# The context vector's lane of the modulation's multiply-adds: from VectorE to GpSimd, as a multiply and an add

## The reference

```python
for l in range(DEPTH):
    mod = silu_c @ w_mod[l] + b_mod[l]
    shift, scale, gate = jnp.split(mod[:, None, :], 3, axis=-1)
    cmod = silu_cc @ w_mod[l] + b_mod[l]
    cshift, cscale, cgate = jnp.split(cmod, 3)
    h = rmsnorm(x, norm_g[l]) * (1.0 + scale) + shift
    hc = rmsnorm(cx, norm_g[l]) * (1.0 + cscale) + cshift
    ...                      # projections, two attention mixers, gate, output projection
    x = x + gate * (y @ w_o[l])
    if with_ctx:
        cx = cx + cgate * (yc @ w_o[l])
```

## Time and profile before

| | |
|---|---|
| median of 3 runs | 2505.77 us (2504.22 to 2507.44) |
| profiled execution | 2506.52 us |
| its span, first to last instruction | 2504.7 us |
| mean granted TensorE clock | 0.992 |
| TensorE matmul busy | 2398.6 us (96%) |
| VectorE busy | 1527.2 us (61%) |
| ScalarE busy | 1033.8 us (41%) |
| GpSimd busy | 232.0 us (9%) |

### The profile page before, as it was taken

How to read it: one execution, slowest core, us unless ns; L and a number is a source line. 1 busy time by engine, 2 the same in 40 slices (tenths; PEclk the granted TensorE clock), 3 DMA queues, 4 the chain that set the end, 5 groups by cost and what they waited for, 6 DMA issues and landing times. The chain is left out here.

```text
span 2504.7 us, 31388 instructions
## 1 busy us (share of the span) xinstructions
PE 2398.6 (96%) x11660; PEld 1919.8 (77%) x11660; DVE 1527.2 (61%) x2575; ACT 1033.8 (41%) x1712; POOL 232.0 (9%) x329
## 2 busy tenths in 40 slices
PE   6899999999999999999899999999999999999998
PEld 1467787877667878887777788978878888899886
DVE  1247766677777877857746556666576544444664
ACT  3232232334343322333353445444544445654543
POOL 0001101001110000002121100100110001101100
PEclk9999999999999999999999999999999999999999
DMA  9756644434333475666465464755655566567653
GB/s 342 283 207 237 211 144 151 167 128 152 103 116 135 143 246 166 202 204 214 158 202 165 129 201 156 263 183 189 201 166 186 185 207 220 169 201 232 191 193 127
DMA packets 231174, 467.96 MB, mean 187 GB/s; under 512 B 17642, under 2 KB 42536, under 8 KB 229744
## 3 DMA queue, kind: packets, MB, share of 16 engines
q1 hardware_dynamic: 209104, 394.94, 47.7%
q0 software_dynamic: 21920, 71.01, 8.8%
HBM read 435.10 MB, written 30.79 MB: 186 GB/s over the span
## 5 line engine op out<-in xcount | busy, mean ns | idle before, releaser
L2091 PE MATMUL pp<-w_hi,hT_hi 128*128 128x512 f32 (+3 forms) x2904 | 1171.0, 403 | 6.7 <-DVE xy L1521 2.8
L2093 PE MATMUL pp<-w_hi,hT_lo 128*128 128x512 f32 (+3 forms) x2904 | 1116.5, 384 | 0.0
L2092 PE MATMUL pp<-w_lo,hT_hi 128*128 128x512 f32 (+3 forms) x2904 | 1114.4, 384 | 0.0
L1491 DVE TENSOR_TENSOR w_lo<-raw,w_hi 128x1024 fp32r<-128x1024 f32 (+4 forms) x570 | 671.9, 1182 | 579.9 <-ACT w_hi L1213 578.6
L1213 ACT ACTIVATE w_hi<-raw 128x1024 fp32r<-128x1024 f32 (+4 forms) x570 | 580.2, 1023 | 446.3 <-PE pp L2093 373.8
L2091 PEld LDWEIGHTS pp<-w_hi,hT_hi 128*128 128x128 f32 x2904 | 547.9, 189 | 136.4 <-issue 38.1
L2093 PEld LDWEIGHTS pp<-w_hi,hT_lo 128*128 128x128 f32 x2904 | 546.6, 188 | 105.8
L2092 PEld LDWEIGHTS pp<-w_lo,hT_hi 128*128 128x128 f32 x2904 | 548.5, 189 | 94.7 <-issue 6.9
L1591 DVE SCALAR_TENSOR_TENSOR arena<-raw,cT,arena 128x512 f32<-128x512 f32 x240 | 172.3, 745 | 0.7
L1591 DVE SCALAR_TENSOR_TENSOR xy<-raw,cT,xy 128x512 f32<-128x512 f32 x180 | 126.7, 744 | 0.0
L1372 ACT ACTIVATE arena<-pY 128x512 f32<-128x512 f32 (+2 forms) x114 | 62.0, 544 | 146.0 <-PE pY L2252 109.0
(11 more groups left out here) (305 smaller groups left out, 1753.0 us busy)
## 6 DMA issues: line engine op xcount, KB each, us to landing
raw<-in_w_mod_dram SPq DMA_DIRECT2D x192, 512.0 KB, 5.3
raw<-in_w_in_dram SPq DMA_DIRECT2D x168, 512.0 KB, 4.2
raw<-in_e_w_in_dram SPq DMA_DIRECT2D x104, 512.0 KB, 4.6
raw<-in_w_o_dram SPq DMA_DIRECT2D x64, 512.0 KB, 4.6
raw<-in_o_w_in_dram SPq DMA_DIRECT2D x64, 512.0 KB, 4.7
raw<-in_w_out_dram SPq DMA_DIRECT2D x64, 512.0 KB, 4.1
raw<-in_w_in_dram SPq DMA_DIRECT2D x56, 440.0 KB, 3.9
scratch_u<-ust POOLq DMA_DIRECT2D x35, 512.0 KB, 4.3
```

Of the source, the lines that this page charges most:

```text
L1491: dve.tensor_tensor(w_lo[:, g.s % SPLIT, 0:n], raw[:, g.n % RAW, 0:n], w_hi[:, g.s % SPLIT, 0:n].bitcast(F32), ALU.subtract).then_inc(lo_d ...
L2091: pe.matmul(dst, hT_hi[:, kk, o:o + P], hi[:, k, :], start=a, stop=False)
L2092: pe.matmul(dst, hT_hi[:, kk, o:o + P], lo[:, k, :], start=False, stop=False)
L2093: ins = pe.matmul(dst, hT_lo[:, kk, o:o + P], hi[:, k, :], start=False, stop=z)
```

## The change

For lane 1 the mac leaves VectorE. GpSimd does it with two instructions: it multiplies the raw K tile in place by the context's column of `cT`, waits for that, and adds the product to the running sum of lane 1 (or to `parts` with K = 0). Since the multiply destroys the raw tile, GpSimd first waits for VectorE's mac of lane 0 on the same tile. Each lane has a semaphore and a count of its own; SP, `bias`, `fold` and `fold_row` wait for both or for the lane that they read. The slots in the plan stay as they are, so the macs of lane 1 stand in GpSimd's queue where they stood in VectorE's. The chunks with lane 0 only stay as they were.

```diff
--- before.py
+++ after.py
@@ -687,10 +687,10 @@
     for todo in plan.at:
         for e in todo:
             if e[0] == "mac":
-                mac_n[e[1:]] = len(mac_n) + 1
+                mac_n[e[1:]] = sum(k[2] == e[3] for k in mac_n) + 1
     side_n = {ch.name: n for n, ch in enumerate(W.sides)}
     for g in W.sided:
-        mac_end[g] = max(mac_n[g.ch.name, K, v] for K in g.ks for v in g.ch.lanes)
+        mac_end[g] = {v: mac_n[g.ch.name, g.ks[-1], v] for v in g.ch.lanes}
     acc_before = {}
     for n, ch in enumerate(W.sides):
         same = [c for c in W.sides[:n] if c.acc == ch.acc]
@@ -779,7 +779,7 @@
         fl_here, fl_added, fl_logged, fl_min, fl_stored = (sem(n) for n in ("fl_here", "fl_added", "fl_logged", "fl_min", "fl_stored"))
 
         cb_here = [sem(f"cb_here{n}") for n in range(2)]
-        parts_clear, side_bias, maced = sem("parts_clear"), sem("side_bias"), sem("maced")
+        parts_clear, side_bias, multiplied, maced = sem("parts_clear"), sem("side_bias"), sem("multiplied"), [sem(f"maced{v}") for v in range(2)]
 
         def at(o, *shape):
             n = int(np.prod(shape))
@@ -858,9 +858,9 @@
             key = ("fold", ch.name, 1) if ch.row is None else ("fold_row", ch.name)
             return filled["O"], left["O", key]
 
-        def maced_all(ch, v=None):
-
-            return maced, max(mac_n[ch.name, ch.ks[-1], w] for w in ch.lanes if v in (None, w))
+        def maced_all(ch, v):
+
+            return maced[v], mac_n[ch.name, ch.ks[-1], v]
 
         def heads_before(m, n):
             return plan.heads[plan.H[m, n].qi - 1] if plan.H[m, n].qi else None
@@ -970,7 +970,8 @@
                     if p.ch.kind == "mod":
                         sp.wait_ge(quanta, p.q1)
                     elif p.ch.kind == "side":
-                        sp.wait_ge(maced, mac_end[p])
+                        for v, n in mac_end[p].items():
+                            sp.wait_ge(maced[v], n)
                     else:
                         sp.wait_ge(lo_done, p.s + 1)
                 ch = g.ch
@@ -1016,10 +1017,34 @@
                 ch, n = C[name], side_n[name]
                 if n:
                     prev = W.sides[n - 1]
-                    pool.wait_ge(maced, mac_n[prev.name, 0, prev.lanes[-1]])
+                    for v in prev.lanes:
+                        pool.wait_ge(maced[v], mac_n[prev.name, 0, v])
                 else:
                     pool.wait_ge(parts_clear, 1)
                 pool.dma_start(parts[0:1, :], D["b_mod"][ch.layer:ch.layer + 1, ch.c0:ch.c0 + 512]).then_inc(side_bias, 16)
+
+            def mac(name, K, v):
+                if v != 1:
+                    return
+                ch = C[name]
+                g = ch.groups[K // GROUP]
+                acc, n = accs[C[name].acc][:, v, :], mac_n[name, K, v]
+                if K % GROUP == 0:
+                    pool.wait_ge(raw_here[g.n % RAW], 16 * (g.n // RAW + 1))
+                if K == 0:
+                    pool.wait_ge(side_bias, 16 * (side_n[name] + 1))
+                    if acc_before[name] is not None:
+                        pool.wait_ge(*folded(acc_before[name]))
+                    elif ch.acc == 2:
+                        pool.wait_ge(*freed_from(plan.U["b", 7, 3].X, ("score", "b", 7, 3)))
+                else:
+                    pool.wait_ge(maced[v], mac_n[name, K - 1, v])
+                k = K % GROUP
+                part = raw[:, g.n % RAW, 512 * k:512 * k + 512]
+                pool.wait_ge(maced[0], mac_n[name, K, 0])
+                pool.tensor_scalar(part, part, cT[:, K, 1:2], None, ALU.mult).then_inc(multiplied, 1)
+                pool.wait_ge(multiplied, mac_n[name, K, 1])
+                pool.tensor_tensor(acc, part, parts[:, :] if K == 0 else acc, ALU.add).then_inc(maced[1], 1)
 
             def gate_store(name):
                 ch = C[name]
@@ -1182,6 +1207,8 @@
                         clear()
                     elif name == "bias":
                         bias(*key)
+                    elif name == "mac":
+                        mac(*key)
                     elif name == "gate":
                         gate(*key)
                     elif name == "tables":
@@ -1574,10 +1601,12 @@
                     scaled_gain(name, key)
 
             def mac(name, K, v):
+                if v != 0:
+                    return
                 ch = C[name]
                 g = ch.groups[K // GROUP]
                 acc, n = accs[C[name].acc][:, v, :], mac_n[name, K, v]
-                if K % GROUP == 0 and v == 0:
+                if K % GROUP == 0:
                     dve.wait_ge(raw_here[g.n % RAW], 16 * (g.n // RAW + 1))
                 if K == 0:
                     dve.wait_ge(side_bias, 16 * (side_n[name] + 1))
@@ -1586,10 +1615,10 @@
                     elif ch.acc == 2:
                         dve.wait_ge(*freed_from(plan.U["b", 7, 3].X, ("score", "b", 7, 3)))
                 else:
-                    dve.wait_ge(maced, mac_n[name, K - 1, v])
+                    dve.wait_ge(maced[v], mac_n[name, K - 1, v])
                 k = K % GROUP
                 dve.scalar_tensor_tensor(acc, raw[:, g.n % RAW, 512 * k:512 * k + 512], cT[:, K, v:v + 1], parts[:, :] if K == 0 else acc,
-                                         ALU.mult, ALU.add).then_inc(maced, 1)
+                                         ALU.mult, ALU.add).then_inc(maced[v], 1)
 
             def sums(name, n):
                 if name == "a":
@@ -2113,8 +2142,8 @@
 
             def fold_row(name):
                 b = begin("O", "fold_row", name)
-                pe.wait_ge(*maced_all(C[name]))
                 for v in C[name].lanes:
+                    pe.wait_ge(*maced_all(C[name], v))
                     ins = pe.matmul(b[32 * v:32 * v + 1, :], ones_mat[:, 0:1], accs[C[name].acc][:, v, :], start=True, stop=True)
                 ins.then_inc(filled["O"], 1)
```

## The result

The changed kernel takes 2621.82 us (median of 4 runs, 2619.25 to 2628.84) against 2505.75 us before: a ratio of 1.0467, 95% interval 1.0446 to 1.0489, or +116 us. The forecast was 2556 us with a range of 2500 to 2650: the sign and the mutual lock held, the time lies in the range, but the loss is 2.3 times what I worked out.

What follows compares the result with a forecast made beforehand. TensorE, 96% busy, was taken to bound the kernel. Window losses of +6, +26, +10 and +8 us gave +50 on the profiled 2506.5 us, 2556.5; the forecast was 2556 us, range 2500 to 2650.

Steps and rivals of the forecast that it cites:

- What bounds the kernel, and the relief: TensorE, 96% busy, sets the end; VectorE loses 129 us of macs, worth at most 10 us on the path.
- The multiply's price: GpSimd's multiply of 128x512: between 0.53 and 0.92 us, taken as 0.7; with an add of 1.2, a pair costs 1.9.
- dear pairs: Rival, chance 0.12: a GpSimd multiply and add cost 2.9 us together, making +153 us, 2659 us.
- its sign: GpSimd's new lines taking 2.5 us or more in mean would show the upper end due.
- The sum by windows: GpSimd pairs, lane 0 macs and splits can't overlap: +6 (163-202 us), +26 (202-268), +10 (268-808), +8 (808-1030).
- The lock, symmetric: GpSimd's reading multiply or add holds off VectorE's macs and splits for up to its whole length, as VectorE does GpSimd.
- Lateness between 268 and 808 us: Attention steps of VectorE start up to 1.2 us late; half of TensorE's 21.5 us idle time added, +10.
- Folds: TensorE's fold of lane 1 comes 2.7 us after the last mac was due; GpSimd's backlog stops TensorE there, 12 times.
- The clock: TensorE's granted clock is 0.99 to 1.00 everywhere, the 2.4 GHz level, so it plays no part.
- Only late, not locked: Rival, chance 0.20: VectorE is never held up, only GpSimd runs late; about +17, 2523 us.
- faster: Rival, chance 0.10: a pair under 1.45 us, the lock costs little, half of 20 us of waits go; 2496 us.
- nothing moves: Rival, chance 0.08: gain and loss cancel within 5 us; 2506 us.

Runs made afterwards that it cites:

- e_free: Changed kernel without lane 1's multiply and add; GpSimd writes eight zeros per tile (512 for K = 0), waits kept: 2493.06 us, 0.9949 of the kernel before.
- e_add_only: Changed kernel without the multiply; GpSimd adds the raw tile itself to lane 1's running sum: 2518.73 us, 1.0044 of the kernel before.
- e_tt_mul: Changed kernel with GpSimd's multiply as a two-input tensor_tensor against the broadcast column of cT: 2596.79 us, 1.0355 of the kernel before.
- e_light: Changed kernel with only four chunks' lane 1 (64 tiles, slots 227 to 435) on GpSimd, the rest on VectorE: 2520.47 us, 1.0048 of the kernel before.
- e_light_memset: Only four chunks (64 tiles, slots 227 to 435) moved, with five zero-writing memsets per tile replacing multiply and add: 2503.11 us, 0.9992 of the kernel before.
- e_memset: Changed kernel with five zero-writing GpSimd memsets per tile replacing lane 1's multiply and add, waits kept: 2548.07 us, 1.0161 of the kernel before.

## Why the prediction went wrong

*What bounds the kernel, and the relief.* Right: TensorE sets the end, and VectorE's relief (120 us, taken as 129) was worth 13 us (10 predicted), shown by `e_free`.

*The multiply's price.* This is the step that failed. I bounded it by a memset and by a memset plus the fixed part of a power op, 0.53 to 0.92 us, and took 0.7; it measured 1.57. Both bounds rest on the pace of writing, and GpSimd's time for an element depended on the operation's form: 1.57, 1.04 and 1.27 us for three instructions on the same 512 elements. With the range of 0.9 to 1.97 for the add the sum's upper end, 2.9 us a pair, took in the measured 2.84 by luck of the add's end, so the case that came true was the one I had called dear pairs, at 0.12 and 2659 us; its sign, 2.5 us or more in mean, came with 1.78 + 1.43. That the price makes the difference between 50 and 116 us is borne out by two runs: `e_add_only` with 1.27 us of instructions a tile lost 10 us and `e_tt_mul` with 2.31 lost 89, which puts my 1.9 us near 60 (an interpolation between kernels whose instructions differ).

*The sum by windows.* With 2.84 in place of 1.9 us my own terms give 14 x 2.84 + 18 - 39 = +19, 31 x 2.84 + 33.6 - 66 = +56, 244 + 314 - 540 + 10 = +28, and 173 + 88 - 222 = +39, in all +142; measured were 0, 42, 34 and 44, +119. So the form of the sum held from the second stretch on. It failed in the first, where I had +6 even at 1.9 us and nothing was lost, and it was too strict for the first two together (+75 against 42): a window's work can be done later than it is due. GpSimd has done 39 of the 45 tiles at 311 us, and the other six are paid in the next stretch, where 91 pairs lie instead of 86.

*The lock, symmetric.* Right that both sides stand, by the rows at 217 us, by `e_light` against `e_light_memset` and by `e_memset` against the change. Too simple in its length: the sum gave every pair its whole length as time in which VectorE stands, and beside the multiply VectorE went on after about 0.5 of 1.57 us. (The trace of before has 24 power ops, not 23; the last, at 2495 us, took 1.10 us where others of its size took 0.71, and fits the same reading.) The lock costs in two ways, which by the interpolations above come to this: it makes GpSimd's pairs longer on the steep part of the curve (3.0 to 3.4 us in the change, some 40 us; 2.5 to 2.9 in `e_tt_mul`, some 20), and it holds up VectorE (some 28 and 49 us). Which is the larger depends on the instructions, and neither was measured by itself.

*Lateness between 268 and 808 us, +10.* Too low: 34 us. 17.3 of it is one wait for the first rotation, whose load and whose weight split both came late by the backlog that the dense window left; I had costed loads behind pairs at nothing. Some of the rest is the lock's (64 tiles: 13 us in `e_light`).

*Folds.* Right in kind: of the twelve, seven waited for GpSimd, 43 us, and one for VectorE, 12 us.

*The clock.* Left out; 33 us of TensorE's longer busy time. It isn't a cause of its own but a surcharge on the idle stretches.

*The rivals.* "Only late, not locked" is refuted by `e_light` against `e_light_memset`, "faster" by the time and, where GpSimd has room, by `e_light`, "nothing moves" by the time.

## What to carry to other kernels

Price a GpSimd instruction by its own form and shape, not by a neighbour's: a scalar multiply of 128x512 cost 1.57 us there, the same as a two-input product 1.04, and VectorE did product and sum together in 0.67. Before work is moved to an idle engine, divide its price by the spacing at which the work is due; near 100% the loss grew here by about 100 us for a microsecond per item (192 items), while 2.34 us an item cost 10 us. And GpSimd beside a VectorE that is busy with two-input instructions wasn't a second engine: where one read the other stood, so the move could pay only as far as neither was waited for.

## What the runs showed of the hardware that I had not expected

GpSimd's memsets, 528 ns for 128x512, did not lengthen a single one of VectorE's macs (longest 0.75 us in `e_memset` and `e_light_memset`), while its reads did, up to 1.78 us in the rows above: it is the reading, not the engine's being busy. The length of an instruction doesn't tell how long it holds VectorE: the multiply of 1.57 us did so for about its first 0.5 us, the add of 1.27 us for all but its last 0.2, and the kernel with the shorter multiply of 1.04 us held VectorE longer (147 against 89 us in all). GpSimd's product with one tile as input and a column as scalar is slower (1569 ns) than its instructions with two inputs (1043 ns for a product with the column broadcast, 1293 for a sum of two full tiles). And after 5.6 us without matmuls TensorE ran at half pace (granted clock 0.50) for 4.8 us, so that gap cost nearly half of its own length again.
